# A mixing stage of eight small heads, its products placed between the weight parts of the projections around it

## The chip, the cores and the metric

One core of one Trainium2 chip runs the whole kernel in one launch. The metric is the device time in microseconds; the kernel before has a median of 1385.91 us over three runs (1381.9 to 1387.32). TensorE (PE) does the matrix products, VectorE (DVE) and ScalarE (ACT) the elementwise work, GpSimd (POOL) little here, and SyncE (SP) issues the weight transfers.

## The reference

Two transformer blocks on 256 tokens of width 1024, all in float32. The stage of this case is the first mixer of the second block. It projects the normed rows to queries, keys and values of two kinds of heads, and multiplies their outputs by an output matrix:

```
def ab_mixer(h, w_in, b_i, b_f, head_gain, w_out):
    mq, mk, mv, mo, mi, mf, sq, sk, sv = _split(h @ w_in, AB_SIZES)
    hm = mlstm(mq, mk * dk ** -0.5, mv, mi + b_i, mf + b_f)
    hm = rmsnorm(hm, head_gain) * sigmoid(mo)
    hs = stick_breaking(sq, sk, sv)
    return concatenate([hm, hs]) @ w_out
```

Four heads are of the mLSTM kind (queries and keys of 64, values of 128): weights of exp(gate sums) times scores, causal, divided by max(|row sum|, exp(-m)), then an rms norm over each head's 128 values, a gain and a sigmoid gate. Four are of the stick-breaking kind (all 128): with z = q k / sqrt(128), the weight of an earlier key is exp(log sigmoid(z) + sum of log sigmoid(-z) over the keys between), which needs a running sum over keys. Behind the stage come the residual sum, cross attention and an MLP.

## The kernel before, in words

Rows are tokens (two tiles of 128) or, in the turned form, columns of 256 tokens. All weights stream from memory once. `weight_plan` lists them as *units* of 1 MB in the order of use; a unit is two *parts* of 128x1024. SyncE loads unit n into one of four slots (`weights_sp`, L248) as soon as the part four units earlier is split. `split` makes of each part a high half on ScalarE (L276) and a low half on VectorE (L279), four parts in the ring, and three matmuls (hi*hi, hi*lo, lo*hi) stand for one product in float32. `cols_part` (L300) takes one part of 128 output columns: 24 matmuls of 256 tokens, output turned. `rows_product` (L362, and L380 for the last two parts, which are taken together, output bank by output bank) has tokens as output rows, 12 matmuls of 512 columns for each part. Its `ready(k)` is called ahead of chunk k, and for the last parts all chunks' `ready` are called before their first matmul. `cols_done` and `rows_done` let ScalarE or VectorE first split a few parts ahead and then wait for a product. Each engine works through its queue in order; semaphores tell of each step.

`ab_pe`, `ab_act` and `ab_dve` write the stage out by hand for the three engines:
- `ab_qk`: six column units give queries and keys of all eight heads, evacuated to `ABT` by ScalarE (L1343) and VectorE in turn; `ab_g` the gates, whose row chain runs on VectorE and ScalarE while TensorE does `ab_vo` (values and output gate of the mLSTM heads, eight parts); `ab_sv` the values of the other heads, four parts.
- Then the eight heads, n = 0 to 3 mLSTM, 4 to 7 stick-breaking, with nothing else on TensorE. `first(n)` (L1295, L1296, or L1299, L1300) gives the outer sum of gates or the scores z. VectorE adds masks (`after_first`: L1431, L1433, or L1436), ScalarE takes exp (L1367) or a soft-plus in three steps (L1371 to L1373). `second(n)` is q k (L1310, L1311), or the running sum by a triangular matrix (L1315, L1316) over VectorE's soft-plus row (L1453). VectorE makes the weights (`after_l`: L1445), or a sum (L1457) whose exp ScalarE takes (L1379). `weigh(n)` (L1327 to L1329) multiplies by the values, and `finish(n)` divides (L1468 to L1473) or copies (L1477) into `OM2`. Each of the three products has two banks of PSUM (0 and 1, 2 and 3, 4 and 5), and step n runs `first(n)`, `second(n-1)`, `weigh(n-2)`.
- VectorE's square sums of the first four heads (L1499, L1500) follow head 4's copy, ScalarE's rsqrt (L1382, L1383) stands behind, and the gates of both token tiles (L1507, L1508) come at the end.
- `turn_pe(6)` transposes all eight chunks (L484), ScalarE and VectorE split them (L494, L510), and `ab_out`, a rows product of eight parts, follows.

## Time and profile before

| | |
|---|---|
| Median of 3 runs | 1385.91 us |
| The profiled execution | 1385.74 us, span 1383.9 us |
| TensorE busy | 1312.2 us, 95% of the span |
| VectorE, ScalarE, GpSimd busy | 59%, 51%, 9% |
| Mean granted clock of TensorE | 0.977 |
| DMA, mean | 148 GB/s |

Times in the profile are in us from the span's start. "Granted clock" is the share of 2.4 GHz at which TensorE was let run; 0.50 is 1.2 GHz. Busy shares of TensorE are of pipelined matmuls with modelled ends, so the start-to-start distance of matmuls tells more than their durations. "x<-y: a, n, b" in a list of waits means that x waited for y for a us in total, n times, at most b us.

### The profile page before, as it was taken

The page shows a single profiled execution, that of the slowest core. Times are in us where ns is not written, and L with a number is a line of the kernel's source. Part 1 is how long each engine was busy: PE and PEld are TensorE (multiplying, and loading weights), DVE is VectorE, ACT ScalarE, POOL GpSimd, SP SyncE. Part 2 cuts the span into 40 slices and gives each one's busy share as a digit, 9 for nine tenths or more (in the row PEclk, how much of TensorE's full clock was granted, in tenths as well). Part 3 has the DMA queues.
Part 4 walks back from the last instruction along what each step waited for, and adds up shares of the span by engine and source line. Part 5 has one row for each costly group of instructions (what it writes and reads, how often), then busy time and mean ns, then how long its engine had stood idle before and what let it go on. Part 6 is the DMA issues. An engine that isn't in the chain of part 4 may idle for free.

```text
span 1383.9 us, 20977 instructions
## 1 busy us (share of the span) xinstructions
PE 1312.2 (95%) x8608; PEld 1191.3 (86%) x8608; DVE 819.2 (59%) x1184; ACT 711.6 (51%) x1129; POOL 128.7 (9%) x138
## 2 busy tenths in 40 slices
PE   7988999999999987999999999999899999999997
PEld 6877799998879866888998888978899888899886
DVE  5766478885456654645554447877655554555444
ACT  6666476664475543645554336554124544555433
POOL 5000001110000000000111000012540000011000
PEclk9999999999999988999999999999899999999999
DMA  9433355555536530543555554532001462455551
GB/s 323 141 108 119 107 176 190 183 183 184 194 124 197 195 111 31 179 147 100 183 183 184 201 193 129 169 133 87 1 32 45 154 214 93 151 183 183 183 197 47
DMA packets 138353, 205.45 MB, mean 148 GB/s; under 512 B 3730, under 2 KB 114706, under 8 KB 138258
## 3 DMA queue, kind: packets, MB, share of 16 engines
q1 hardware_dynamic: 138258, 204.11, 44.8%
q8 instruction: 68, 1.11, 0.3%
q14 instruction: 27, 0.22, 0.0%
HBM read 203.05 MB, written 1.05 MB: 147 GB/s over the span
## 4 chain that ended last, share of the span: by engine, by line
PE 83%; DVE 9%; ACT 5%; issue 2%; DMA 0%; POOL 0%; DVEq 0%; ACTq 0%
PE ps L300 39%; PE ps L362 26%; PE ps L380 6%; DVE weights_lo L279 2%; PE ps L1925 2%; PE ps L1939 2%; ACT weights_hi L276 1%; PE ps L1936 1%; PE ps L1594 1%; PE ps L1953 1%; PE ps L1616 1%; PE ps L484 1%; ACT normed L900 1%; DVE split_arena L515 1%; ACT normed L404 1%
## 5 line engine op out<-in xcount | busy, mean ns | idle before, releaser
L279 DVE TENSOR_TENSOR weights_lo<-weights,weights_hi 128x1024 fp32r<-128x1024 f32 x379 | 468.4, 1248 | 278.6 <-ACT weights_hi L276 276.6
L300 PE MATMUL ps<-split_arena,weights_hi 128*128 128x256 f32 x2928 | 539.7, 287 | 6.8 <-DVE split_arena L515 6.0
L276 ACT ACTIVATE weights_hi<-weights 128x1024 fp32r<-128x1024 f32 x379 | 396.8, 1057 | 271.8 <-PE ps L362 196.6
L300 PEld LDWEIGHTS ps<-split_arena,weights_hi 128*128 128x128 f32 x2928 | 463.0, 194 | 12.6 <-issue 9.1
L300 PE MATMUL ps<-split_arena,weights_lo 128*128 128x256 f32 x1464 | 417.3, 285 | 0.0
L362 PE MATMUL ps<-weights_hi,split_arena 128*128 128x512 f32 x1040 | 289.4, 395 | 5.4 <-DVE split_arena L1050 1.7
L300 PEld LDWEIGHTS ps<-split_arena,weights_lo 128*128 128x128 f32 x1464 | 284.3, 194 | 0.0
L362 PEld LDWEIGHTS ps<-weights_hi,split_arena 128*128 128x128 f32 x1040 | 194.6, 189 | 51.0 <-issue 9.9
L362 PE MATMUL ps<-weights_lo,split_arena 128*128 128x512 f32 x520 | 161.6, 391 | 0.0
L362 PEld LDWEIGHTS ps<-weights_lo,split_arena 128*128 128x128 f32 x520 | 98.2, 189 | 20.8
L1774 POOL TENSOR_TENSOR normed<-normed 128x512 f32<-128x512 f32 x32 | 34.1, 1065 | 484.8 <-ACTq L1766 484.8
L380 PE MATMUL ps<-weights_hi,split_arena 128*128 128x512 f32 x208 | 66.4, 391 | 0.0
L1782 DVE TENSOR_TENSOR split_arena<-normed,split_arena 128x512 fp32r<-128x512 f32 x32 | 22.1, 692 | 73.8 <-POOL normed L1774 73.8
L1175 POOL TENSOR_TENSOR arena<-arena 128x512 f32<-128x512 f32 x11 | 21.9, 1993 | 274.1 <-ACT arena L1120 179.2
L1764 ACT ACTIVATE normed<-ps 128x512 f32<-128x512 f32 x32 | 19.1, 597 | 53.5 <-PE ps L300 53.5
L1158 DVE SCALAR_TENSOR_TENSOR arena<-ps,conv_cols,arena 128x255 f32<-128x255 f32 (+1 forms) x88 | 38.4, 478 | 13.7 <-ACT arena L1132 12.9
L380 PEld LDWEIGHTS ps<-weights_hi,split_arena 128*128 128x128 f32 x208 | 39.0, 188 | 8.3 <-issue 0.2
L2030 ACT ACTIVATE arena<-ps 128x512 f32<-128x512 f32 x24 | 14.3, 597 | 53.7 <-PE ps L1925 53.7
L1132 ACT ACTIVATE arena<-ps,conv_cols 128x256 f32<-128x256 f32 x44 | 22.4, 560 | 37.8 <-PE ps L300 37.8
L300 PE MATMUL ps<-mem_t_hi,weights_hi 128*128 128x256 f32 x128 | 37.6, 294 | 3.3 <-DVE weights_lo L279 3.3
L380 PE MATMUL ps<-weights_lo,split_arena 128*128 128x512 f32 x104 | 40.5, 389 | 0.0
L515 DVE SCALAR_TENSOR_TENSOR split_arena<-ps,ln_cols,split_arena 128x256 fp32r<-128x256 f32 x72 | 29.4, 476 | 16.8 <-ACT split_arena L498 16.8
(335 smaller groups left out, 1471.0 us busy)
## 6 DMA issues: line engine op xcount, KB each, us to landing
weights<-in_mlp_w SPq DMA_DIRECT2D x64, 1024.0 KB, 5.3
weights<-in_w_up SPq DMA_DIRECT2D x22, 1024.0 KB, 5.1
weights<-in_c_w_in SPq DMA_DIRECT2D x16, 1024.0 KB, 5.4
weights<-in_w_in SPq DMA_DIRECT2D x14, 1024.0 KB, 5.5
weights<-in_ab_w_in SPq DMA_DIRECT2D x12, 1024.0 KB, 5.2
weights<-in_w_down SPq DMA_DIRECT2D x11, 1024.0 KB, 4.9
weights<-in_xa_wv SPq DMA_DIRECT2D x8, 1024.0 KB, 4.9
weights<-in_xa_wq SPq DMA_DIRECT2D x8, 1024.0 KB, 5.7
```

The source lines that it names most:

```text
L276: act.activation(h, r, ACT.Copy).then_inc(s_hi, 1)
L279: dve.tensor_tensor(l, r, h.bitcast(F32), ALU.subtract).then_inc(s_lo, 1)
L300: mm = pe.matmul(o, w[:, k, :], x[:, k, :], start=(k == 0 and i == 0), stop=(k == DC - 1 and i == 2))
L362: mm = pe.matmul(PS[:, banks[nb * t + b], :], x[:, t * P:(t + 1) * P], w[:, c:c + 512], start=(k == 0 and i == 0), stop=False)
L380: mm = pe.matmul(PS[:, banks[nb * t + b], :], x[:, t * P:(t + 1) * P], w[:, c:c + 512], start=(k == 0 and i == 0), stop=(k == chunks - 1 a ...
L515: ins = dve.scalar_tensor_tensor(out=dst[1][:, k, :], in0=PS[:, turn_bank(m) + c2, c * T:(c + 1) * T], scalar=ln_cols[:, gain, k:k + 1], i ...
L1132: ins = act.activation(CS[:, u % 4, f, :], PS[:, G + u % 4, f * T:(f + 1) * T], ACT.Identity, bias=c[:, 3:4], scale=c[:, 2:3])
L1158: ins = dve.scalar_tensor_tensor(out=CS[:, u % 4, f, lag:T], in0=PS[:, G + u % 4, f * T:(f + 1) * T - lag], scalar=c[:, tap:tap + 1], in1= ...
L1774: pool.tensor_tensor(RSQ[:, u % 2, :, :], RLU[:, u % 2, :, :], RLU[:, u % 2, :, :], ALU.mult).then_inc(named("m1_f"), 1)
L1782: dve.tensor_tensor(HID[1][:, 2 * u:2 * u + 2, :], RSQ[:, u % 2, :, :], HID[0][:, 2 * u:2 * u + 2, :].bitcast(F32), ALU.subtract).then_inc ...
L1925: mm = pe.matmul(PS[:, gi % 2, j * P:(j + 1) * P], LT[:, gi, j, :], XI[:, gi, j, :], start=True, stop=True)
L1939: mm = pe.matmul(PS[:, 4 + gi % 2, j * P:(j + 1) * P], YI[:, gi, j, :], XT[:, gi, j, :], start=True, stop=True)
```

## The change

The stage has no stretch of its own any more. The plan's order becomes: queries and keys of the mLSTM heads (`ab_mqk`, two units), gates, `ab_vo`, then queries and keys of the stick-breaking heads (`ab_sqk`, four units), their values, and the output matrix. From `ab_sqk` on, the work is cut into steps s: 0 to 7 are the parts of `ab_sqk`, 8 to 11 those of `ab_sv`, 12 to 19 those of `ab_out`. Behind part s TensorE calls `after(s)`, which issues the `first`, `second`, `weigh` and `turn` that the tables `FIRST_AT`, `SECOND_AT`, `AB_WEIGH_AT` and `AB_TURN_AT` give for it (step: head). ScalarE and VectorE split part s+3 at each step and then do what their tables give.

Further: each small product has one bank (4, 5, 6), and the transposes have bank 7, so each waits for the reading of the head before. `weigh` of heads 4 to 7 has its operands exchanged and gives the turned output with two matmuls; `out_high` and `out_low` split it straight from PSUM into the operand of `ab_out`. Only the four chunks of the mLSTM heads are transposed (`turn`, `high`, `low`). The square sums stand at step 7, the gates at steps 8 and 9, the transposes at steps 10 and 11. The output product waits for its chunks one by one. U3 and L3 lie in the normed rows' tile.

```diff
-    cols("ab_qk", "ab_w_in", range(0, 1536, 256))
+    cols("ab_mqk", "ab_w_in", (1024, 1280))
     plan.append(("ab_g", "gates", "half", 128))
     rows("ab_vo", "ab_w_in", DC, 1536)
+    cols("ab_sqk", "ab_w_in", (0, 512, 256, 768))
     rows("ab_sv", "ab_w_in", DC, 2560, 512)
     rows("ab_out", "ab_w_out", DC)
...
-        SUM_BANKS = {"w_out": WB, "down": range(A, A + 4), "c_out": (2, 3, 0, 1)}
+        SUM_BANKS = {"w_out": WB, "down": range(A, A + 4), "ab_out": (2, 3, 0, 1),
...
+        SQK_TILE = (0, 4, 2, 6)
+        NSL = 12
+        FIRST_AT = {0: 0, 1: 1, 2: 2, 3: 3, 5: 4, 6: 5, 9: 6, 11: 7}
+        SECOND_AT = {0: 0, 1: 1, 2: 2, 3: 3, 7: 4, 8: 5, 11: 6, 13: 7}
+        AFTER_L_AT = {1: 0, 2: 1, 3: 2, 4: 3, 6: 4, 7: 5, 10: 6, 12: 7}
+        EXP_W_AT = {7: 4, 8: 5, 13: 6, 14: 7}
+        AB_WEIGH_AT = {2: 0, 3: 1, 4: 2, 5: 3, 13: 4, 14: 5, 15: 6, 16: 7}
+        AB_FINISH_AT = {3: 0, 4: 1, 5: 2, 6: 3}
+        AB_SSQ_AT, AB_GATE_AT = 7, {8: 0, 9: 1}
+        AB_TURN_AT = {10: 0, 11: 2}
...
+            def free_m(u):
+                if u == 0:
+                    pe.wait_ge(named("xk_a"), 2)
+                    pe.wait_ge(named("xk_d"), 3)
+            for u in range(2):
+                cols_unit("ab_mqk", u, HT, A + u, free_m, turned(5, pe))
+            cols_unit("ab_g", 0, HT, A + 3)
+            rows_product("ab_vo", chunk(HT), DC)
...
+                    pe.wait_ge(named("ab_ca"), 1)
+                    pe.wait_ge(named("ab_cd"), 1)
+                    pe.wait_ge(named("xk_a"), 3)
+                elif n == 4:
+                    pe.wait_ge(named("ab_ca"), 3)
+                elif n == 6:
+                    pe.wait_ge(named("ab_ca"), 5)
+                if n:
+                    pe.wait_ge(named("ab_u"), n)
...
             def second(n):
-                b = 2 + n % 2
-                if n >= 2:
-                    pe.wait_ge(named("ab_sec_read"), n - 1)
+                if n:
+                    pe.wait_ge(named("ab_sec_read"), n)
...
             def weigh(n):
-                b = 4 + n % 2
                 pe.wait_ge(named("ab_w"), n + 1)
-                if n >= 2:
-                    pe.wait_ge(named("ab_o"), n - 1)
+                if n:
+                    pe.wait_ge(named("ab_o"), n)
...
+                else:
+                    if n == 4:
+                        pe.wait_ge(named("ab_svr"), 2)
+                    v = slice((n - 4) * P, (n - 3) * P)
+                    pe.matmul(PS[:, 6, 0:T], SV[:, 0, v], w[:, 0:T], start=True, stop=False)
+                    mm = pe.matmul(PS[:, 6, P:T], SV[:, 1, v], w[:, T:384], start=False, stop=True)
                 mm.then_inc(named("ab_pv"), 1)
...
-            for n in range(10):
-                if n < 8:
-                    first(n)
-                if 1 <= n <= 8:
-                    second(n - 1)
-                if n >= 2:
-                    weigh(n - 2)
+            def turn(c):
+                pe.wait_ge(named("ab_om"), 2)
+                if c:
+                    pe.wait_ge(named("ab_tl"), 1)
+                else:
+                    pe.wait_ge(named("ab_row"), 5)
+                for i in range(2):
+                    for t in range(TT):
+                        mm = pe.transpose(PS[:, 7, i * T + t * P:i * T + (t + 1) * P],
+                                          OM2[:, t, (c + i) * P:(c + i + 1) * P], ident[:, :])
+                mm.then_inc(named("ab_tp"), 1)
+
+            def after(s):
+                if s in FIRST_AT:
+                    first(FIRST_AT[s])
+                if s in SECOND_AT:
+                    second(SECOND_AT[s])
+                if s in AB_WEIGH_AT:
+                    weigh(AB_WEIGH_AT[s])
+                if s in AB_TURN_AT:
+                    turn(AB_TURN_AT[s])
+
+            for u in range(4):
+                for f in range(2):
+                    if f == 0:
+                        pe.wait_ge(named(("ab_va", "ab_sgm")[u % 2]), u // 2 + 1)
+                    cols_part(first_unit["ab_sqk"] + u, f, HT, u)
+                    after(2 * u + f)
+
+            def sv_ready(k):
+                if k % 2 == 0 and 2 <= k <= 6:
+                    after(8 + k // 2 - 1)
+            rows_product("ab_sv", chunk(HT), DC, width=512, ready=sv_ready,
+                         free=lambda: pe.wait_ge(named("ab_ca"), 3))
+            after(NSL - 1)
+
+            def out_ready(k):
+                if k:
+                    after(NSL + k - 1)
+                if k < 4:
+                    pe.wait_ge(named("ab_tl"), k // 2 + 1)
+                else:
+                    pe.wait_ge(named("ab_o"), k + 1)
+
+            def out_free(t):
+                if t == 0:
+                    pe.wait_ge(named("ab_ca"), 5)
+                else:
+                    pe.wait_ge(named("ab_svr"), 2)
+            rows_product("ab_out", ab_t, DC, ready=out_ready, free_tile=out_free, banks=SUM_BANKS["ab_out"])
...
+            def exp_w(n):
+                act.wait_ge(named("ab_sec_read"), n + 1)
+                act.wait_ge(named("ab_pv"), n - 1)
+                act.activation(W3[:, n % 2, :], U3[:, n % 2, :], ACT.Exp).then_inc(named("ab_w"), 1)
...
+            def out_high(n):
+                act.wait_ge(named("ab_pv"), n + 1)
+                act.activation(ab_t(0, n), PS[:, 6, 0:T], ACT.Copy).then_inc(named("ab_oh"), 1)
+
+            base = first_part[first_unit["ab_sqk"]]
+            for s in range(NSL + DC - 1):
+                split(act, base + s + 3)
+                if s < 8 and s % 2:
+                    u, tile = s // 2, SQK_TILE[s // 2]
+                    act.wait_ge(s_used, base + s + 1)
+                    act.activation(ABT[:, tile:tile + 2, :], PS[:, u, :].rearrange("p (c n) -> p c n", c=2), ACT.Copy,
+                                   scale=(1.0 if tile >= 4 else P ** -0.5)).then_inc(named("ab_ca"), 1)
+                if s == NSL - 1:
+                    for t in range(TT):
+                        rows_done(act, "ab_sv", t)
+                        act.activation(SV[:, t, :], PS[:, G + t, :], ACT.Copy).then_inc(named("ab_svr"), 1)
+                if s in EXP_W_AT:
+                    exp_w(EXP_W_AT[s])
+                if s in AB_WEIGH_AT and AB_WEIGH_AT[s] >= 4:
+                    out_high(AB_WEIGH_AT[s])
+                if s in FIRST_AT:
+                    soft(FIRST_AT[s])
+                if s == AB_SSQ_AT:
                     act.wait_ge(named("ab_ssq"), 1)
                     act_then(act.activation(HST[:, 1, :], HST[:, 0, :], ACT.Ln, bias=eps_c[:, 0:1], scale=1.0 / P))
                     act.activation(HST[:, 2, :], HST[:, 1, :], ACT.Exp, scale=-0.5).then_inc(named("ab_hrs"), 1)
+                if s in AB_TURN_AT:
+                    high(AB_TURN_AT[s])
...
+            def after_second(n):
+                dve.wait_ge(named("ab_second"), n + 1)
+                dve.wait_ge(named("ab_sp"), n - 3)
+                dve.scalar_tensor_tensor(out=U3[:, n % 2, :], in0=PS[:, 5, 0:384], scalar=-1.0,
+                                         in1=U3[:, n % 2, :], op0=ALU.mult,
+                                         op1=ALU.add).then_inc(named("ab_sec_read"), 1)
 
...
+            def low(c):
+                dve.wait_ge(named("ab_th"), c // 2 + 1)
+                dve.tensor_tensor(ab_group(1, c), PS[:, 7, :].rearrange("p (c n) -> p c n", c=2),
+                                  ab_group(0, c).bitcast(F32), ALU.subtract).then_inc(named("ab_tl"), 1)
+
+            def out_low(n):
+                dve.wait_ge(named("ab_oh"), n - 3)
+                dve.tensor_tensor(ab_t(1, n), PS[:, 6, 0:T], ab_t(0, n).bitcast(F32),
+                                  ALU.subtract).then_inc(named("ab_o"), 1)
+
+            base = first_part[first_unit["ab_sqk"]]
+            for s in range(NSL + DC - 1):
+                split(dve, base + s + 3)
+                if s in AFTER_L_AT:
+                    after_l(AFTER_L_AT[s])
+                if s in FIRST_AT:
+                    after_first(FIRST_AT[s])
+                if s in SECOND_AT and SECOND_AT[s] >= 4:
+                    after_second(SECOND_AT[s])
+                if s in AB_FINISH_AT:
+                    finish(AB_FINISH_AT[s])
+                if s == AB_SSQ_AT:
                     dve.wait_ge(named("ab_o"), 4)
-                    head_squares_dve(OM2[:, :, 0:512], HSQ, HST, 4, "ab_ssq")
-                if n == 8:
+                    head_squares_dve(OM2, HSQ, HST, 4, "ab_ssq")
+                if s in AB_GATE_AT:
                     dve.wait_ge(named("ab_hrs"), 1)
                     dve.wait_ge(named("gate_gain"), 2)
-                    for t in range(TT):
-                        head_gate_dve(OM2[:, :, 0:512], t, HST, 4, SGM, "ab_om")
+                    head_gate_dve(OM2, AB_GATE_AT[s], HST, 4, SGM, "ab_om")
+                if s in AB_TURN_AT:
+                    low(AB_TURN_AT[s])
+                if s in AB_WEIGH_AT and AB_WEIGH_AT[s] >= 4:
+                    out_low(AB_WEIGH_AT[s])
...
-            turn_pe(6, OM2, lambda t, h: (pe.wait_ge(named("ab_om"), t + 1), pe.wait_ge(named("ab_o"), 8)))
-            rows_product("ab_out", chunk(HT), DC, ready=turned(6, pe))
```

How this moves rows on TensorE. Before, behind the last values' matmuls (L380), the heads start (L1295: `first`, L1310: `second`, L1327: `weigh`):

```order
L380 MATMUL ps<-weights_lo,split_arena 128x512
L380 MATMUL ps<-weights_hi,split_arena 128x512
L1295 MATMUL ps<-arena,sel 128x256 [waits ab_svr,ab_row,ab_sgm,ab_va]
L1296 MATMUL ps<-arena,sel 128x128
L1295 MATMUL ps<-arena,sel 128x256
L1296 MATMUL ps<-arena,sel 128x128
L1310 MATMUL ps<-arena 128x256
L1311 MATMUL ps<-arena 128x128
L1295 MATMUL ps<-arena,sel 128x256 [waits ab_u]
L1296 MATMUL ps<-arena,sel 128x128
L1310 MATMUL ps<-arena 128x256
```

After, step 1: behind a part of `ab_sqk` (L301) come head 1's `first` (L1311) and `second` (L1325), then the next part:

```order
L301 MATMUL ps<-split_arena,weights_hi 128x256 x2
L301 MATMUL ps<-split_arena,weights_lo 128x256
L1311 MATMUL ps<-arena,sel 128x256 [waits ab_u]
L1312 MATMUL ps<-arena,sel 128x128
L1325 MATMUL ps<-arena 128x256 [waits ab_sec_read]
L1326 MATMUL ps<-arena 128x128
L301 MATMUL ps<-split_arena,weights_hi 128x256 [waits weights_lo_ready,ab_sgm]
L301 MATMUL ps<-split_arena,weights_hi 128x256
```

And after, around steps 9 and 10: the end of the second values part (L363), head 6's `first` (L1315), four transposes (L1362), and the last two values parts (L381):

```order
L363 MATMUL ps<-weights_lo,split_arena 128x512
L363 MATMUL ps<-weights_hi,split_arena 128x512
L1315 MATMUL ps<-arena 128x256 [waits ab_u,ab_ca,weights_lo_ready]
L1316 MATMUL ps<-arena 128x128
L1362 MATMUL ps<-ident,arena 128x128 [waits ab_row,ab_om]
L1362 MATMUL ps<-ident,arena 128x128 x3
L381 MATMUL ps<-weights_hi,split_arena 128x512
L381 MATMUL ps<-weights_lo,split_arena 128x512
```

Each small product now has a part's matmuls ahead of it, except between steps 9 and 10, and its waits hold up the parts behind it.

VectorE before, at the square sums (L1499, L1500), behind head 4's copy (L1477) and ahead of head 6's sum (L1436), with no weight part split in the stage:

```order
L1453 SCALAR_TENSOR_TENSOR arena<-arena 128x384 [waits ab_l]
L1457 SCALAR_TENSOR_TENSOR arena<-ps,arena 128x384 [waits dve_chain,ab_second]
L1477 COPY arena<-ps 128x2x128 [waits ab_pv]
L1499 TENSOR_TENSOR arena<-arena 128x512 [waits ab_o]
L1500 TENSOR_REDUCE arena<-arena 128x4 [waits dve_chain]
L1499 TENSOR_TENSOR arena<-arena 128x512 [waits dve_chain]
L1500 TENSOR_REDUCE arena<-arena 128x4 [waits dve_chain]
L1436 TENSOR_TENSOR arena<-ps,neg_gt 128x384 [waits dve_chain,ab_w,ab_first]
L1453 SCALAR_TENSOR_TENSOR arena<-arena 128x384 [waits ab_second,ab_l]
L1457 SCALAR_TENSOR_TENSOR arena<-ps,arena 128x384 [waits dve_chain,ab_second]
```

VectorE after, the same place (L1599, L1600: square sums; L280: low half of a part; L1545: head 5's sum; L1607, L1608: a gate; L1522: head 6's masked scores):

```order
L1599 TENSOR_TENSOR arena<-arena 128x512 [waits ab_o]
L1600 TENSOR_REDUCE arena<-arena 128x4 [waits dve_chain]
L1599 TENSOR_TENSOR arena<-arena 128x512 [waits dve_chain]
L1600 TENSOR_REDUCE arena<-arena 128x4 [waits dve_chain]
L280 TENSOR_TENSOR weights_lo<-weights,weights_hi 128x1024 [waits dve_chain,weights_hi_ready]
L1545 SCALAR_TENSOR_TENSOR normed<-ps,normed 128x384 [waits ab_sp,ab_second]
L1607 TENSOR_TENSOR arena<-arena 128x512 [waits gate_gain,ab_hrs]
L1608 TENSOR_TENSOR arena<-arena 128x512 [waits dve_chain]
L280 TENSOR_TENSOR weights_lo<-weights,weights_hi 128x1024 [waits weights_hi_ready]
L1522 TENSOR_TENSOR normed<-ps,neg_gt 128x384 [waits ab_w,ab_first]
L1607 TENSOR_TENSOR arena<-arena 128x512 [waits gate_gain,ab_hrs]
L1608 TENSOR_TENSOR arena<-arena 128x512 [waits dve_chain]
```

The gates come before the last four heads are done instead of behind them, and the low halves stand between.

## Rows read from the trace of the kernel before

**Rows 1.** The page's part 4: the chain that ended last, by engine.
```profile
PE 83%; DVE 9%; ACT 5%; issue 2%; DMA 0%; POOL 0%; DVEq 0%; ACTq 0%
```

**Rows 2.** Windows: us; PE, PEld, DVE, ACT, POOL busy; PEclk; DMA share; GB/s.
```profile
439.00:461.96 22.96, 22.96 (x193) 22.96 (x193) 11.11 (x11) 10.27 (x11) 0.00 (x0) 1.00 0.59 194
...
484.88:496.04 11.16, 11.15 (x50) 8.93 (x48) 4.95 (x5) 6.37 (x7) 1.28 (x1) 1.00 0.52 183
496.04:540.34 44.30, 31.05 (x128) 24.82 (x129) 25.41 (x60) 15.17 (x29) 0.00 (x0) 0.75 0.10 36
540.34:563.01 22.67, 22.67 (x97) 18.75 (x98) 11.04 (x13) 9.29 (x16) 0.00 (x0) 0.97 0.36 118
```

**Rows 3.** Waits from 496.04 to 540.34: total us, times, longest.
```profile
ACT arena L1371 <- DVE arena L1436: 9.5, 4, 3.6
...
PE ps L1315 <- DVEq L1455: 8.6, 4, 4.0
```

**Rows 4.** Timeline of PE: start, us, engine, line, operation.
```profile
484.32 0.39 PE L380 MATMUL ps<-weights_hi,split_arena 128*128 128x512 f32 x1
484.64 0.31 PE L1280 MATMUL ps<-ident,arena 36*128 36x36 f32 x2
...
512.88 0.60 PE L1299 MATMUL ps<-arena 128*128 128x256 f32 x2
513.31 0.39 PE L1300 MATMUL ps<-arena 128*128 128x128 f32 x2
...
516.13 0.38 PE L1316 MATMUL ps<-arena,ones 128*128 128x128 f32 x2
516.35 0.39 PE L1327 MATMUL ps<-arena 128*128 128x129 f32 x2
...
537.37 2.75 PE L484 MATMUL ps<-ident,arena 128*128 128x128 f32 x16 [2.17 <-DVE arena L1477]
```

**Rows 5.** Groups by line from 484 to 563.1: busy us, mean ns of one.
```profile
L279 DVE TENSOR_TENSOR weights_lo<-weights,weights_hi 128x1024 fp32r<-128x1024 f32 x12 | 14.5, 1224 | 19.2 <-ACT weights_hi L276 19.1
L276 ACT ACTIVATE weights_hi<-weights 128x1024 fp32r<-128x1024 f32 x12 | 12.4, 1056 | 12.5 <-PE ps L362 12.5
...
L1445 DVE TENSOR_TENSOR arena<-ps,arena 128x384 f32<-128x384 f32 x4 | 2.2, 557 | 2.2 <-PE ps L1311 1.3 <-ACT arena L1367 0.9
...
L1367 ACT ACTIVATE arena<-arena 128x384 f32<-128x384 f32 x4 | 2.1, 523 | 7.7 <-DVE arena L1433 7.6
...
L1431 DVE SCALAR_TENSOR_TENSOR arena<-ps,arena,neg_ge 128x256 f32<-128x256 f32 x4 | 1.9, 479 | 0.9 <-PE ps L1296 0.9
...
L1433 DVE SCALAR_TENSOR_TENSOR arena<-ps,arena,neg_ge 128x128 f32<-128x128 f32 x4 | 1.4, 340 | 0.0
```

**Rows 6.** Timeline of DVE, 513.0 to 536.
```profile
513.08 0.16 DVE L1468 SCALAR_TENSOR_TENSOR arena<-ps,arena 128x2 f32<-128x2 f32 x1 [0.24 <-PE ps L1329]
...
513.66 0.61 DVE L1473 TENSOR_SCALAR arena<-ps,arena 128x128 f32<-128x128 f32 x2
...
521.70 0.68 DVE L1499 TENSOR_TENSOR arena<-arena 128x512 f32<-128x512 f32 x1
...
534.15 0.68 DVE L1507 TENSOR_TENSOR arena<-arena 128x512 f32<-128x512 f32 x1
```

**Rows 7.** Windows around idle places; columns as in rows 2.
```profile
412.60:415.60 3.00, 0.11 (x1) 0.00 (x0) 2.97 (x5) 2.24 (x6) 0.00 (x0) 0.97 0.00 0
415.60:419.00 3.40, 3.33 (x16) 3.34 (x17) 2.09 (x5) 1.64 (x4) 0.00 (x0) 0.52 0.60 190
513.70:515.40 1.70, 0.00 (x0) 0.02 (x1) 1.50 (x4) 0.60 (x2) 0.00 (x0) 1.00 0.00 0
515.40:518.80 3.40, 2.43 (x14) 1.93 (x14) 2.03 (x7) 1.58 (x3) 0.00 (x0) 1.00 0.00 0
...
525.40:535.00 9.60, 7.88 (x26) 6.20 (x26) 3.55 (x8) 3.07 (x7) 0.00 (x0) 0.50 0.00 0
```

**Rows 8.** The page's part 6: a DMA issue, KB, us to landing.
```profile
weights<-in_ab_w_in SPq DMA_DIRECT2D x12, 1024.0 KB, 5.2
```

172 lines of the change are left out of this document (65 added, 107 removed).

## Prediction

> **What bounds the kernel now.** I read the page first, then the stretch of this stage in a table of windows, then the waits inside it, and last single rows for durations. The page says that TensorE is the bound over the whole: 83% of the chain that ended last [rows 1]. So the time is TensorE's own work plus its idle stretches, and a change can gain only where TensorE is idle or slow. The windows show one place where it is both [rows 2]: the projections before this stage run at full clock without a gap (22.96 of 22.96 us), and so do the values (11.16 us) and the output product (22.67 us), but the 44.30 us between have a mean clock of 0.75 and move 36 GB/s of weights. TensorE's busy time of 31.05 us there is inflated by overlapping, modelled ends and by the low clock. The waits of that stretch run from engine to engine [rows 3]: TensorE waits for VectorE's soft-plus rows (8.6 us in four waits) and ScalarE for VectorE's masked scores (9.5 us). Eight heads pass through three engines, and nothing else is queued to fill the gaps.
>
> **The change, part by part.** The eight heads' small products are no longer by themselves; each small group stands between two weight parts of the projections. I take as a common start the end of the value-and-gate projection (484.88 us of the trace before, where all eight q,k parts already lie behind; in the new order they lie ahead).
>
> Before, from that start plus the eight parts: 22.96 + 11.16 + 44.30 + 22.67 = 101.09 us [rows 2].
>
> After, TensorE's own work at full clock:
> - Projections: 22.96 + 11.16 + 21.97 = 56.09 us. The last is 22.67 less 0.70, since its mean clock was 0.97 and 3% of it are lost to that.
> - Small products. Start to start at full clock, a 128x256 takes 0.43 us and a 128x128 or 128x129 0.22 [rows 4] (512.88 to 513.31; 516.13 to 516.35); a 128x384 I take as both, 0.65. Eight of `first` at 0.65 make 5.2; four of `second` at 0.65 and four at 0.87 make 6.1; four of `weigh` at 0.66 and, with the new form of two matmuls for the last four heads (256 and 128 columns), four at 0.65 make 5.2; eight transposes instead of sixteen at 0.17 (2.75 us for 16, [rows 4]) make 1.4. Together 17.9 us. The last four heads now come out of `weigh` already turned, so their eight transposes go.
>
> The ceiling of the gain is thus 101.1 - 56.1 - 17.9 = 27.1 us. What is taken from it is TensorE's new idle time. For that I walk the three queues in their new order with the durations of [rows 5, 6], allowing 0.05 us for a flag between engines and 0.21 us from the last column of a product to its reader. A weight part costs TensorE 2.87 us, ScalarE 1.03 (its hi half) and VectorE 1.20 (its lo half; start to start they come a little under the durations of single ones, 1.06 and 1.22), and each step asks for all three. Times below count from the common start; the parts are numbered from 0.
> - **Steps 0 and 1.** ScalarE is free at 1.8 (its table load for exp and ln ends 1.78 after the start before, and it does the same here). hi 2 and 3 end at 3.8, lo 3 at 5.3, then VectorE takes head 0's sum (0.79) to 6.05, ScalarE its exp to 6.6 and hi 4 to 7.65, VectorE lo 4 to 8.9 and the weights of head 0 to 9.5. TensorE wants to start `second` of head 1 in the single bank 5 at 7.7 and can at 9.6: **1.9 us idle**. Before there were two banks for it; now one, so head 1 waits until head 0 is read.
> - **Steps 2 to 4.** The same circle takes 4.8 us a step on TensorE (2.87 + three small groups) and about 4.5 round the others, so it just holds (0.1 idle). But `weigh` has one bank too: head 1's waits until VectorE has finished head 0 (a chain of 1.19 us, [rows 6], 513.08 to 514.27), done at 20.9 where TensorE is ready at 19.3: **1.6 us**.
> - **Step 5.** VectorE waits for head 4's `first` before it finishes head 2, though that could have been done: its sum 0.55, the finish 1.19, done at 30.6; TensorE ready at 28.7: **2.1 us**.
> - **Steps 7 to 10.** The heaviest place. VectorE does the square sums of the first four heads in one piece (2.86 us: four operations of 0.69 with 0.03 between, [rows 6]) from 40.8 to 43.7; ScalarE waits for them with its rsqrt (0.52) ahead of hi 11, which ends at 45.3; lo 11 ends at 46.5. TensorE, which takes the last two value parts together, has been ready since 45.0: **1.65 us**. Between step 9 and step 10 no projection stands on TensorE, since both are called ahead of those two parts. Step 10's transposes need the gates of both token tiles; VectorE queues lo 11, head 5's sum (0.56), gate 0 (1.41, two operations of 0.69 [rows 6]), lo 12, head 6's sum, gate 1, done at 51.9. TensorE is ready at 47.3: **4.7 us**.
> - **Steps 11 to 18.** ScalarE and VectorE have room (hi, lo, one exp, a copy and a subtraction: 2.0 and 2.2 us against TensorE's 3.4). I get 0.3 + 0.35 us, for the value bank's copy and head 7's soft-plus.
>
> Sum of the idle time 12.7 us. **Clock:** [rows 7] show that an idle stretch of 1.7 us (513.7 to 515.4) is followed by full clock, while one of 3.0 us (412.6 to 415.6) is followed by 0.52; with solid work behind it, the low level held for 3.4 us, so it cost 1.7. Only the 4.7 us place is of that kind: **1.7 us**. **Handovers** that no row shows in this mixture: TensorE's switches between weight parts and small groups. The nearest row is the one at 484.64, which started 0.10 after the matmul of 484.32 had had 0.22 us [rows 4]. From below they cost 0 (inside the stage 516.35 follows 516.13 without a gap, though it is another product), from above 0.1 at each of some 40 switches, 4 us. I take the near value for the ten that also wait for another engine: **1.0 us**.
>
> After: 56.1 + 17.9 + 12.7 + 1.7 + 1.0 = 89.4 us against 101.1, a gain of 11.7 us. The profiled execution took 1385.74 us, which is also within 0.2 of the median of the runs (1385.91), so **1374.0 us**.
>
> Edits at nothing: the new order of the weight transfers (they are the same units; the rate while TensorE is fed is 183 to 194 GB/s [rows 2], and it now goes on instead of pausing), U3 and L3 in the normed rows' place (that tile is unused here), the banks moved by one, the gate rows' chain, which the value-and-gate projection covers as before. Cover gone: before, the 44 us let the weight ring fill. If it is needed later, the next idle place comes sooner, but TensorE was busy through all 22.67 us of the product behind, with transfers at only 118 GB/s [rows 2].
>
> A rule that speaks against the change: the Trainium skill, TensorE: Matmul & The Clock Gate, section "A second HAM failure mode: psum-queue depth-cycling", describes a kernel in which small idles between groups of matmuls, each harmless, make the clock swing between its two levels. This trace agrees in one half only: full clock held through 515.4 to 518.8 with 2.43 of 3.40 us busy [rows 7]. By that rule the result would be the last rival below.
>
> **Rivals.**
> - *The walk is pessimistic.* VectorE and ScalarE follow closer, or the handovers are free and the idle at step 10 meets no low clock: idle near 11 to 12 us and nothing on top, a gain of 14 to 17, 1369 to 1372. For it: rounded durations in a chain of some 30 links; at 0.95 and 1.00 for hi and lo the walk gives 10.2 us idle. Against it: a mean hi and lo of 1.06 and 1.22.
> - *The circle doesn't hold.* In steps 2 to 4 only 0.3 us a step are in hand. If each link costs 0.1 more and handovers reach their upper bound, idle and handovers come to 15 + 4, the clock falls twice (3.4): 96.5 us, a gain of 4 to 5, about 1381.
> - *The change does not bring what it moves.* The time comes back behind the stage because the ring is no longer full: the 44 us of slack held up to four units; two late transfers of 5.2 us each [rows 8] would leave some 1.3 us, 1384.5.
> - *Slower: the low clock spreads.* If the idles of 1.6 to 2.1 us at steps 1, 4 and 5, one after another, bring the clock to 1.2 GHz and it stays there until the stage ends, the parts cost double. The gain before clock (13.4 us) is gone as soon as 13.4 us of full-speed work runs at the low level; if all of steps 1 to 11 do (some 30 us of projections and 12 of small products, less 12 idle that is absorbed) it costs 30 us: about 1402. For it: 9.60 us ran at 0.50 with TensorE busy for 7.88 of them (525.4 to 535.0, [rows 7]), in small products with idle between; against it: a part of 2.87 us without a gap stands in every step, and such work brought the clock back after the idle of 412.6.
>
> **How the numbers follow.** My forecast (1372 to 1378) 0.55; the walk pessimistic 0.22; the circle not holding 0.12; the time coming back 0.05; low clock spreading 0.06. Within 0.5% (7 us, what a measurement of this kernel can tell) means above 1379. The forecast and the pessimistic walk count as faster (0.77); of the third case, which stretches from 1378 to 1383, 0.05 lie below 1379 and 0.07 above; the fourth lies in the middle band, with 0.01 of the last. That gives 0.82 faster, 0.13 same, 0.05 slower. The range holds the first two cases and most of the third: 1368.5 to 1381.
>
> **What would show it.** In the profile after, each of the idle places by name: TensorE waiting for VectorE's weights row at head 1's `second`, for the finishes at heads 1 and 3, and at the transposes for the gates, the longest, near 5 us, followed by a few us of low clock. The stretch from the value-and-gate projection's end to the output product's end should be 87 to 92 us, with no window at a mean clock under 0.9 but that one. I am wrong if TensorE waits more than 3 us at any other step, if the wait at the transposes is under 3 us, or if the stages behind are longer than before by over 1 us.

## The result, and the profile after

The changed kernel takes 1370.53 us (median of 4 runs, 1369.25 to 1371.36) against 1386.18 us for the kernel before on the same chip: a ratio of 0.9892, 95% interval 0.9875 to 0.991, so 15.7 us less. A second set on another chip gave 1371.88 against 1385.46, 0.9906 (0.989 to 0.9923). The forecast was 1374.0, range 1368.5 to 1381, with 0.82 on faster.

The windows of the profile after (us; busy time of PE, PEld, DVE, ACT, POOL; PEclk; DMA share; GB/s) show the projections ahead of the stage, the stage with values and output product in it, its step 9 and 10, what follows that place, the rest of the stage, and all that lies behind:

```profile
437.90:460.85 22.95, 22.95 (x107) 18.73 (x105) 15.26 (x23) 12.66 (x16) 1.29 (x1) 1.00 0.61 194
460.85:548.75 87.90, 79.14 (x451) 68.44 (x450) 49.64 (x83) 40.30 (x63) 1.29 (x1) 0.96 0.35 120
505.00:512.89 7.89, 2.75 (x13) 1.83 (x12) 5.96 (x8) 4.21 (x8) 0.00 (x0) 0.91 0.40 134
512.89:523.27 10.38, 10.38 (x40) 8.52 (x41) 4.13 (x6) 3.99 (x7) 0.00 (x0) 0.74 0.29 101
523.27:548.75 25.48, 25.48 (x120) 21.12 (x119) 14.35 (x19) 13.39 (x24) 0.00 (x0) 1.00 0.42 144
...
548.75:1367.50 818.75, 787.62 (x5181) 719.21 (x5179) 457.43 (x576) 393.37 (x600) 87.11 (x72) 0.99 0.43 141
```

Against [rows 2] the stretch that was 22.96 + 11.16 + 44.30 + 22.67 us (the same windows of the kernel before, cut where the next product's first matmul starts, give 100.92) is now 87.90. The transfers run on at 120 GB/s where they had stood at 36. Of the profiled pair's 16.5 us, 13.0 lie here, 1.1 ahead of the stage (its first projection matmul comes at 460.85; in the old order the same place is 484.88 less the 22.96 of the eight parts, 461.92) and 2.3 behind it (821.06 to 818.75); the experiments come back to that last part. The 1.1 us are no gain of the change that these runs can show: in the executions of the kernels below, which have the same work ahead of it, that place lies anywhere from 459.80 to 461.56, and in another one of the kernel before at 461.22.

**Idle or slow?** The time of the stretch splits into three: TensorE's waits of more than 0.1 us (from its timeline), what the low clock costs (half of the time at 1.2 GHz outside these waits), and the rest, which is TensorE's own work at full clock. Before it is 13.3 + 10.6 + 77.1 us, after it 8.8 + 2.7 + 76.4. So of the 13.0 us only 4.5 are waits that are gone, and 7.9 are low clock that is gone. Before, the low level set in behind short waits already and held through ten us of small products without a gap (kernel before, columns as above; the waits ahead of 500.71 are 0.89 and 1.40 us):

```profile
496.04:500.71 4.67, 2.39 (x12) 1.93 (x12) 3.07 (x5) 2.51 (x4) 0.00 (x0) 1.00 0.27 109
500.71:511.00 10.29, 10.29 (x31) 8.23 (x32) 5.42 (x18) 2.07 (x4) 0.00 (x0) 0.50 0.31 104
```

TensorE's waits inside the stretch, from its timeline (start, us, engine, line, operation, and in brackets the idle time before it with what ended it). Of the old ring, [rows 3], none is left; these are all that exceed 0.1 us:

```profile
470.16 0.70 PE L1325 MATMUL ps<-arena 64*128 64x256 f32 x2 [0.58 <-DVEq L1533]
...
482.44 0.46 PE L1343 MATMUL ps<-arena 128*128 128x129 f32 x2 [1.19 <-DVE arena L1559]
...
492.28 0.46 PE L1343 MATMUL ps<-arena 128*128 128x129 f32 x2 [1.84 <-DVE arena L1559]
507.87 0.70 PE L1315 MATMUL ps<-arena 128*128 128x256 f32 x2 [1.04 <-DVE weights_lo L280]
512.89 1.11 PE L1362 MATMUL ps<-ident,arena 128*128 128x128 f32 x4 [4.10 <-DVE arena L1608]
```

They are the five places that the walk of the queues named: head 1's `second`, `weigh` of heads 1 and 3 behind VectorE's finishes, the low half at step 9, and the transposes behind the gates. The ones of 0.3 and 0.35 us at steps 11 to 18 did not come, nor did the 0.1 in steps 2 to 4. VectorE's timeline up to the last one reads as it was laid out: low half, head 5's sum, gate 0, low half, head 6's scores, gate 1, each behind the other with only 0.21 us of idle time between, ahead of the second low half:

```profile
506.59 1.23 DVE L280 TENSOR_TENSOR weights_lo<-weights,weights_hi 128x1024 fp32r<-128x1024 f32 x1 [1.62 <-ACT weights_hi L277]
507.73 0.55 DVE L1545 SCALAR_TENSOR_TENSOR normed<-ps,normed 128x384 f32<-128x384 f32 x1
508.20 0.68 DVE L1607 TENSOR_TENSOR arena<-arena 128x512 f32<-128x512 f32 x1
508.92 0.69 DVE L1608 TENSOR_TENSOR arena<-arena 128x512 f32<-128x512 f32 x1
509.82 1.22 DVE L280 TENSOR_TENSOR weights_lo<-weights,weights_hi 128x1024 fp32r<-128x1024 f32 x1 [0.21 <-ACT weights_hi L277]
510.96 0.55 DVE L1522 TENSOR_TENSOR normed<-ps,neg_gt 128x384 f32<-128x384 f32 x1
511.43 0.68 DVE L1607 TENSOR_TENSOR arena<-arena 128x512 f32<-128x512 f32 x1
512.15 0.69 DVE L1608 TENSOR_TENSOR arena<-arena 128x512 f32<-128x512 f32 x1
```

### The profile page after: what moved, and what is told of

Read it like the earlier page. It is cut to its first block, busy times and chain, and to the rows that moved or that the text cites. A ratio compares the mean times of both kernels' runs of the same rounds, so it can differ in the third digit from the quotient of the medians.

```text
span 1367.5 us, 20948 instructions
## 1 busy us (share of the span) xinstructions
PE 1299.7 (95%) x8592; PEld 1180.7 (86%) x8592; DVE 813.0 (59%) x1180; ACT 711.7 (52%) x1133; POOL 130.6 (10%) x138
## 4 chain that ended last, share of the span: by engine, by line
PE 83%; DVE 9%; ACT 5%; issue 2%; DMA 0%; POOL 0%; DVEq 0%; ACTq 0%
PE ps L301 38%; PE ps L363 26%; PE ps L381 6%; DVE weights_lo L280 2%; PE ps L2025 2%; ACT weights_hi L277 2%; PE ps L2039 2%; PE ps L2036 1%; PE ps L1694 1%; PE ps L2053 1%; PE ps L1716 1%; PE ps L485 1%; ACT normed L902 1%; DVE split_arena L516 1%; ACT normed L405 1%
## 5 line engine op out<-in xcount | busy, mean ns | idle before, releaser
L280 DVE TENSOR_TENSOR weights_lo<-weights,weights_hi 128x1024 fp32r<-128x1024 f32 x379 | 468.5, 1248 | 269.9 <-ACT weights_hi L277 268.0
L301 PE MATMUL ps<-split_arena,weights_hi 128*128 128x256 f32 x2928 | 536.0, 286 | 7.0 <-DVE split_arena L516 6.1
L301 PEld LDWEIGHTS ps<-split_arena,weights_hi 128*128 128x128 f32 x2928 | 458.7, 192 | 13.1 <-issue 9.8
L301 PE MATMUL ps<-split_arena,weights_lo 128*128 128x256 f32 x1464 | 414.9, 283 | 0.0
L363 PE MATMUL ps<-weights_hi,split_arena 128*128 128x512 f32 x1040 | 289.8, 395 | 5.2 <-DVE split_arena L1052 1.7
L301 PEld LDWEIGHTS ps<-split_arena,weights_lo 128*128 128x128 f32 x1464 | 281.6, 192 | 0.0
L363 PEld LDWEIGHTS ps<-weights_hi,split_arena 128*128 128x128 f32 x1040 | 194.1, 189 | 49.9 <-issue 9.0
L363 PE MATMUL ps<-weights_lo,split_arena 128*128 128x512 f32 x520 | 162.0, 391 | 0.0
L363 PEld LDWEIGHTS ps<-weights_lo,split_arena 128*128 128x128 f32 x520 | 98.0, 189 | 20.7
L381 PE MATMUL ps<-weights_hi,split_arena 128*128 128x512 f32 x208 | 68.2, 400 | 0.0
L381 PEld LDWEIGHTS ps<-weights_hi,split_arena 128*128 128x128 f32 x208 | 40.2, 193 | 8.7 <-issue 0.2
L1160 DVE SCALAR_TENSOR_TENSOR arena<-ps,conv_cols,arena 128x255 f32<-128x255 f32 (+1 forms) x88 | 38.4, 478 | 13.7 <-ACT arena L1134 12.9
L381 PE MATMUL ps<-weights_lo,split_arena 128*128 128x512 f32 x104 | 41.3, 397 | 0.0
L301 PE MATMUL ps<-mem_t_hi,weights_hi 128*128 128x256 f32 x128 | 38.0, 297 | 3.3 <-DVE weights_lo L280 3.3
```

Source lines behind the costliest of these rows:

```text
L280: dve.tensor_tensor(l, r, h.bitcast(F32), ALU.subtract).then_inc(s_lo, 1)
L301: mm = pe.matmul(o, w[:, k, :], x[:, k, :], start=(k == 0 and i == 0), stop=(k == DC - 1 and i == 2))
L363: mm = pe.matmul(PS[:, banks[nb * t + b], :], x[:, t * P:(t + 1) * P], w[:, c:c + 512], start=(k == 0 and i == 0), stop=False)
L381: mm = pe.matmul(PS[:, banks[nb * t + b], :], x[:, t * P:(t + 1) * P], w[:, c:c + 512], start=(k == 0 and i == 0), stop=(k == chunks - 1 a ...
L1160: ins = dve.scalar_tensor_tensor(out=CS[:, u % 4, f, lag:T], in0=PS[:, G + u % 4, f * T:(f + 1) * T - lag], scalar=c[:, tap:tap + 1], in1= ...
```

## The experiments

All start from the changed kernel. "Stretch" is what the windows above show as 87.90: from the end of the value-and-gate projection, with the eight parts behind it, to the first matmul of the next product. The last column splits it as above: waits, low clock outside them, TensorE's own work. Ratios are against runs of the kernel before on the same chip; the kernels were not all timed on one chip, so between two of them the ratios compare better than the times.

| kernel | us | ratio to before (95%) | stretch, mean clock | waits + low clock + own work |
|---|---|---|---|---|
| before | 1384.1 to 1386.2 | 1 | 100.92, 0.88; again 104.33, 0.84 | 13.3 + 10.6 + 77.1; again 12.6 + 14.9 + 76.8 |
| changed | 1370.53 | 0.9892 (0.9875 to 0.991) | 87.90, 0.96 | 8.8 + 2.7 + 76.4 |
| changed, again | 1371.88 | 0.9906 (0.989 to 0.9923) | 89.54, 0.94 | 8.8 + 4.5 + 76.3 |
| not interleaved | 1394.26 | 1.0068 (1.0053 to 1.0084) | 107.32, 0.84 | 18.0 + 12.8 + 76.5 |
| not interleaved, two `weigh` banks | 1385.29 | 1.0005 (0.9992 to 1.0017) | 103.46, 0.85 | 13.7 + 13.3 + 76.5 |
| transposes after the values | 1363.74 | 0.9855 (0.9841 to 0.9868) | 83.96, 0.98 | 5.6 + 1.7 + 76.7 |
| two `weigh` banks | 1366.77 | 0.9874 (0.9856 to 0.9892) | 86.48, 0.94 | 6.4 + 4.1 + 76.0 |
| squares in two | 1369.04 | 0.9887 (0.987 to 0.9903) | 85.03, 0.98; again 86.56, 0.96 | 7.1 + 1.7 + 76.2; again 7.1 + 3.4 + 76.1 |
| those three | 1360.60 | 0.9829 (0.9811 to 0.9847) | 77.92, 1.00 | 1.4 + 0 + 76.5 |
| bank for the second `second` | 1368.23 | 0.9889 (0.9863 to 0.9915) | 87.52, 0.96 | 8.2 + 3.1 + 76.2 |
| all four | 1358.97 | 0.9816 (0.98 to 0.9832) | 77.29, 1.00; again 77.26, 1.00 | 0.8 + 0 + 76.4; again the same |

**Not interleaved.** Everything of the change stays but the placing:

```diff
-            def after(s):
+            def after(part):
+                if part != NSL - 1:
+                    return
+                for s in range(NSL + DC - 1):
                     ...
```

and likewise on ScalarE and VectorE, whose splits for the parts behind come after the heads' work.

> All small products, sums and exps of the eight heads, in the order of the step tables, stand behind the last values part and ahead of the output product; banks, the turned form of the last four heads' weights-times-values, the halved transposes and the plan's order stay as in the changed kernel. My theory (the gain is the projections that lie between the small products): nearly all of the gain goes; by the stage before (44.3 us alone, less some 4 us for transposes and splits saved, plus waits for single banks) 1382 to 1392 us. Rival (the turned form, four chunks fewer to transpose and to split, and the output product's chunk-by-chunk start bring much of it): 1378 us or less.

Measured: 1394.26 us, 2 above the range, and slower than the kernel before. The rival is out: without the projections between, the turned form and the halved transposes save nothing on balance. The stretch is 19.4 us longer than the changed kernel's, 9.2 of it waits and 10.1 low clock, and 6.4 (or 3.0, by the second profile) longer than before. The same edit with a second bank for `weigh` asked what costs that:

> The kernel without interleaving (all small work behind the last values part), now with two banks for weights-times-values of the first four heads. That kernel's stretch was 107.3 us against 100.9 before, with 17.1 against 11.9 us lost to the low clock, and 4.6 us of TensorE's waits for finishes. Theory (single banks are what makes the other edits of the change cost time where nothing covers them): 3 to 6 us less than without the second bank, 1388 to 1391 us. Rival (the order of the step tables and the gates ahead of the transposes cost it): within 1 us of it, 1394.

Measured: 1385.29 us, 9 less and even with the kernel before; the stretch shrank by 3.9 us, its waits by 4.3. So the single `weigh` bank costs 4.3 us of waits here, where it costs 2.4 in the interleaved kernel (the experiment after the next): the interleaving hides a part of that price. Of the 7.2 us between the two profiled executions, another 4.3 lie behind the stage (821.47 against 817.22 us), a spread that the section on that part tells of and that I don't put down to the bank.

This kernel and the interleaved one with two `weigh` banks differ in the placing alone, 103.46 against 86.48 us in the stretch. One thing stays open: the kernel that is not interleaved keeps the order of the step tables, which was made for the interleaving, with the transposes ahead of the last heads (they wait 3.30 us for the gates there). An order made for a stage by itself could be better; the kernel before is the only one here that has such an order, and it is no faster.

**Transposes after the values.** `turn(0)` and `turn(2)` stand at step 11 ahead of the other products, the second in bank 6, with `high` and `low` ahead of the heads' other work in their engines' step 11:

```diff
-        AB_TURN_AT = {10: 0, 11: 2}
+        AB_TURN_STEP = NSL - 1
...
             def after(s):
+                if s == AB_TURN_STEP:
+                    turn(0)
+                    turn(2)
```

> The transposes of the first four heads' chunks stand behind the last two values parts (step 11) instead of ahead of them, in two banks, nothing else changed. Theory: the 4.1 us wait of TensorE for the gates disappears behind those parts' 5.5 us, and the low clock of 512.9 to 518 with it; about 1 us of it comes back where the output product's first chunk waits for its halves: 1365 us (4.5 to 5.5 less than the changed kernel). Rival a (the wait only moves to the output product's start): 1369 to 1371. Rival b (the clock stays low there for another reason): some 1.7 us less gained, 1367.

Measured: 1363.74 us, 1.3 below the theory's 1365, and a stretch 3.9 us shorter. TensorE's waits from there on, and the clock of the whole stretch:

```profile
510.06 0.70 PE L1315 MATMUL ps<-arena 128*128 128x256 f32 x2 [1.05 <-DVE weights_lo L280]
518.30 0.88 PE L1330 MATMUL ps<-arena,tri 128*128 128x384 f32 x2 [0.31 <-DVE arena L1541]
519.99 0.70 PE L363 MATMUL ps<-weights_hi,split_arena 128*128 128x512 f32 x2 [0.59 <-issue]
```
```profile
461.56:545.52 83.96, 78.39 (x450) 67.85 (x449) 49.40 (x83) 40.10 (x63) 1.29 (x1) 0.98 0.37 125
```

The 4.10 us are gone, 0.9 came back, and no low clock follows; both rivals are out. The 2% that are still lost are another piece of low clock, from 473 us on, told of below.

**Two banks for `weigh`** (heads 1 and 3 in bank 7, `finish` reads from there):

```diff
-                if n:
-                    pe.wait_ge(named("ab_o"), n)
+                if n >= 4:
+                    pe.wait_ge(named("ab_o"), n)
+                elif n >= 2:
+                    pe.wait_ge(named("ab_o"), n - 1)
+                b = 6 + n % 2
```

> Weights-times-values of heads 1 and 3 go to the free bank 7, so they wait for the reading two heads before. Theory: the waits of 1.2 and 1.8 us for VectorE's finishes go, and VectorE's queue then gives back a little at step 8: 2 to 3 us less than the changed kernel, 1368 us. Rival (VectorE's work is the bound in these steps, so another wait takes their place): within 1 us of the changed kernel, 1370.5.

Measured: 1366.77 us. Both waits for finishes are gone, and the wait for the low half at step 9 rose from 1.04 to 1.69 us:

```profile
506.76 0.70 PE L1315 MATMUL ps<-arena 128*128 128x256 f32 x2 [1.69 <-DVE weights_lo L280]
511.79 1.12 PE L1367 MATMUL ps<-ident,arena 128*128 128x128 f32 x4 [4.10 <-DVE arena L1613]
```

That is 3.03 less and 0.65 more, 2.4 us of waits; the stretch shows 1.4, with its clock at 0.94 instead of 0.96. The intervals of the two ratios overlap, so that the rival is out rests on the waits.

**Squares in two** (first token tile at step 6, second at 7, rsqrt at 8):

```diff
-        AB_SSQ_AT, AB_GATE_AT = 7, {8: 0, 9: 1}
+        AB_RS_AT, AB_SSQ_AT, AB_GATE_AT = 8, {6: 0, 7: 1}, {8: 0, 9: 1}
```

> The square sums of the first four heads are done for the first token tile at step 6 and for the second at step 7, and ScalarE's rsqrt stands one step later, so that no low half waits behind 2.9 us of sums. Theory: the wait of 1.0 us for a low half at step 9 goes and the wait for the gates shrinks by some 0.4: 1.5 to 2 us less than the changed kernel, 1368.8 us. Rival (the wait at the gates grows by what is saved ahead of it): 1370 to 1371.

Measured: 1369.04 us; the wait of 1.04 gone, the one at the transposes 3.46 instead of 4.10. The waits are as the theory has them, but the time alone doesn't tell it from its rival: the intervals of this kernel and the changed one overlap.

**All three, and all four.**

> The three edits together: transposes behind the last values parts, two banks for weights-times-values of the first four heads, square sums in two. Theory (the waits are separate places of TensorE's queue, and with all three VectorE has room again): the gains add, since the walk of the queues gives 3.5 us of idle left of 11.8; the stretch from the value-and-gate projection to the end of the output product comes to 77 to 79 us (87.9 in the changed kernel), the time to 1360 us. Rival (VectorE is the bound of the whole stretch, so they don't add): no better than the transposes' edit alone, 1363 to 1364 us.

> The three edits together (transposes behind the last values parts, two banks for weights-times-values, square sums in two) and the second bank for head 1's second product. Theory: 0.65 us less in the stretch than the three (77.3 us, the step-1 wait gone), which is under what the times can tell: 1360 us. Rival (the walk's): the wait comes back at the next steps, 77.9 us as before.

Measured: 1360.60 and 1358.97 us, both better than either kernel. The windows of the two stretches:

```profile
460.99:538.91 77.92, 76.48 (x451) 66.42 (x449) 49.31 (x83) 40.00 (x63) 1.29 (x1) 1.00 0.40 135
```
```profile
459.80:537.09 77.29, 76.45 (x451) 66.38 (x450) 49.30 (x83) 40.01 (x63) 1.29 (x1) 1.00 0.40 136
```

TensorE is busy 76.48 of 77.92 us and never slow: VectorE, busy for 49, is not the bound of the stretch. The gains in waits add, since each wait was its own place in TensorE's queue: 3.2, 2.4 and 1.7 us one by one, 7.3 at once. With the shorter waits the low clock went too. With waits of 0.25 and 0.59 us as the only ones left in the kernel with all four, its stretch gives what TensorE needs by itself: 77.29 - 0.84 = 76.4 us.

**The bank of the first wait.** Head 1's `second` in bank 7:

```diff
+                b = 7 if n == 1 else 5
...
-                    pe.wait_ge(named("ab_sec_read"), n)
+                    pe.wait_ge(named("ab_sec_read"), n - (n == 2))
```

> Head 1's second product goes to the free bank 7, so it doesn't wait until head 0's is read, nothing else changed. What the prediction said (the single bank makes the first wait): TensorE's wait of 0.6 us at step 1 goes, about 1 us faster than the changed kernel. Rival, from the walk with this bank (the circle of sum, exp, high half, low half and weights through ScalarE and VectorE is late by itself): the wait moves to head 2's second product, which waits for the same reading one step later, and the time stays, 1370.5 us.

Measured: 1368.23 us, too wide to tell (1367.23 to 1375.0). The timelines can: head 1's `second` starts 8.66 us after the stretch's start instead of 9.31, head 2's 13.42 instead of 14.06, so the 0.65 us are kept. The prediction's reason holds, and the walk with the durations of single operations, which made the rival, was wrong here.

**Behind the stage.** The changed kernel again, and three kernels with one more execution each:

> The changed kernel once more, beside the others on the same chip: 1370.5 us, 0.989 of the kernel before. If the part of the gain that lies behind the stage (2.3 us in the profiled pair) is the clock's chance phase, the stages behind it will differ again, by up to 5 us, and not always in the same direction; if it is the change's (transfers, buffers), they are again 2.3 us shorter than before's 821.1.

> The kernel before once more, one look. Behind the stage the same instructions run in every kernel of this study, yet they took 816.4 to 821.5 us, the longer the more of them ran at the low clock. If that is chance from execution to execution, this one may take anything in that span; if it goes with the kernel (where its stages lie in time), it takes 821.1 again, as the changed kernel took 818.75 and 818.76.

> The kernel with the square sums in two once more, one look. Chance: anything from 816 to 822 us behind the stage. Bound to the kernel: 821.4 again. The stretch itself 85.0 us again, but for one low-clock piece more or less (1.7 us).

> The kernel with all four edits once more, one look. Chance: anything from 816 to 822 us behind the stage. Bound to the kernel: 819.5 again. The stretch 77.3 us again, since it had no low clock and two short waits.

Measured: 1371.88 us, and the three single ones 1388.28 (before), 1366.72 (squares in two) and 1360.95 (all four). Behind the stage: changed 818.76 us (818.75 the first time), before 820.95 (821.06), squares in two 817.18 (821.36), all four 820.91 (819.51). The first two pairs looked bound to the kernel; the other two show that it is not, since the same kernel differs by 4.2 us from one execution to the other. The two windows of the squares kernel:

```profile
546.04:1367.40 821.36, 788.73 (x5181) 720.43 (x5179) 461.22 (x576) 393.51 (x600) 85.48 (x72) 0.99 0.43 140
```
```profile
547.72:1364.90 817.18, 786.42 (x5181) 718.50 (x5179) 457.66 (x576) 393.45 (x600) 87.17 (x72) 0.99 0.43 141
```

The count of matmuls is the same, 5181. Half of the time at the low level makes 10.2 us of clock lost in the first and 6.8 in the second, without the last 2 to 5 us of the span, where the level is low too and TensorE has nothing to do. Over all kernels 10.2 lost goes with 819.5 to 821.5 us, 8.5 with 818.8, 6.8 with 817.2 to 817.4, 5.1 with 816.4. So the 2.3 us of the first pair are no gain of the change that these runs can show. What sets the number of low pieces there stays open.

## Why the prediction was right

- **Where the gain comes from.** Right: the 44.3 us alone were the only place, and without interleaving the gain is gone (ratio 1.0005 with the banks doubled, 1.0068 without). What the prediction doesn't say is that more of it is clock than idle time: 7.9 us against 4.5.
- **TensorE's own work: 74.0 us.** The kernel without waits shows 76.4. The prediction puts handovers at 1.0 on top, with 4 as an upper bound, but switches between parts and small groups are not the main reason: the kernels that are not interleaved, with hardly a switch, come to 76.5 as well. The rows of the kernel with all four edits show where the 2.4 lie. `first` and `second` of heads 0 to 3 have operands of 4 and 64 rows and take 0.85 us each from start to start, where 0.65 had been taken from a row with 128 (1.6 us in eight groups; the trace of before had it, 0.85 us from 511.26 to 512.11). The eight parts of `ab_sqk` take 24.04 us where they took 22.96 in one piece, and 23.13 in the kernel that is not interleaved, so about 1 us there are switches. The value and output parts take 0.5 more. The rest takes 0.7 less, 0.5 of it the transposes: their 0.17 came from a row (537.37 in [rows 4]) whose 2.75 us ran at a mean clock of 0.67.
- **Idle time: 12.7 us.** It is 0.58 + 1.19 + 1.84 + 1.04 + 4.10 = 8.75 us, at the places named. The first was sized worst (1.9), and mostly from the other side: TensorE was ready for it at 8.73 us from the stretch's start, where the walk had 7.7, since its own work was sized too small; the weights were there at 9.31, where the walk had 9.6. That 0.3 is VectorE, whose operations follow one another closer than their single durations say (the low half 1.15 us to the next operation where 1.20 had been taken). Likewise the circle of steps 2 to 4 held with room because TensorE took 5.44 us for a step that was walked at 4.8. Two of the waits also don't follow from the walk's own times: 30.6 less 28.7 is 1.9 and not 2.1, 46.5 less 45.0 is 1.5 and not 1.65.
- **Clock: 1.7 us.** After the wait of 4.10 us, 10.38 us ran at a mean of 0.74, which is 2.7 us lost. In the second profile of the changed kernel, and in the one with the transposes moved, the clock fell at another wait too, where the prediction allowed no window under 0.9. The reading of [rows 7], that only idle stretches near 3 us are followed by the low level, was wrong for the kernel before already, as the rows of 496 to 511 us above show.
- **Sum.** 76.4 + 8.75 + 2.7 = 87.9 us, as measured; forecast 89.4. That it comes so close is in part luck, since the errors cancel: own work 2.4 more, less 1.0 foreseen, idle 4.0 less, clock 1.0 more.
- **From 11.7 to 15.7 us.** 1.3 of the difference is the stretch (13.0 us). Another 0.3 lies in the medians, 1386.18 where the first runs of before gave 1385.91. The profiled pair adds 1.1 ahead and 2.3 behind, neither of them shown to be the change's. Before's own stretch was 100.92 us in the profile that I worked from and 104.33 in another, with more low clock, and after's 87.90 and 89.54: by which two are paired, the gain of the stretch is 11.4 to 16.4 us. How much of the rest is each can't be told from so few profiles; the second set's 13.6 us fits a smaller sum.
- **Rivals.** The time did not come back behind the stage. The low clock did not spread: the rule that the prediction weighed (the Trainium skill, TensorE: Matmul & The Clock Gate, section "A second HAM failure mode: psum-queue depth-cycling"), of small idles between groups, did show itself, at waits of 0.6 to 1.2 us in some executions, but each piece cost 1.7 us and ended. In the kernel before, though, it held for the ten us behind 500.71, at a cost of 5.1 us. "The circle doesn't hold" is wrong. The result, 1370.5 and 1371.9 us, lies not in the forecast's 1372 to 1378 but in the 1369 to 1372 of "the walk is pessimistic". That rival is right on the idle time and wrong on the rest: it foresaw 11 to 12 us of it and nothing on top, and there were 8.75, with 2.7 of clock and 2.4 of own work on top.

## What to carry to other kernels

A chain of small steps through three engines, which leaves the matrix engine idle or at its low clock for half of the time (13.2 and 9.9 of 44.3 us here), gives that time back only if other matmuls stand between the steps; banks, transposes and forms alone gained nothing here. Count both parts: of the 13.0 us that the stretch became shorter, 4.5 were waits and 7.9 the low clock that had come with them. Walk the three queues in the new order with durations from the trace: it named all five remaining waits, and three small edits at these (an item moved behind a part that hides it, a second bank, a long piece cut in two) brought another 10 us, 1360.6 against 1370.5. Count start to start, not single durations, and take each group's price from a row of its own shape and at full clock: here eight groups with few rows were 0.2 us dearer than the row they were priced by, and since such an error shifts the time at which the matrix engine is ready, it comes back in every wait.
